# Second layer's experts: a group of h is transposed and evicted one weight piece later

## The reference

```python
g, idx = lax.top_k(jnp.swapaxes(aff, 1, 2), cap)      # cap = 128 tokens for each expert
xe = hf[flat].reshape(b, N_EXPERTS, cap, d)           # gather, d = 1024
a = jnp.einsum('becd,edf->becf', xe, w_gate)          # f = 1408
u = jnp.einsum('becd,edf->becf', xe, w_up)
y = jnp.einsum('becf,efd->becd', jax.nn.silu(a) * u, w_down)
y = y * g[..., None]
out = jnp.zeros((b * n, d), y.dtype).at[flat].add(y.reshape(-1, d))
```

## Time and profile before

| | |
|---|---|
| median of 3 runs | 3465.7 us |
| the profiled execution | 3464.97 us |
| its span (first to last instruction) | 3463.2 us |
| outside the span | 1.8 us |
| mean granted TensorE clock | 0.934 of 2.4 GHz |
| TensorE busy | 3005.9 us (87%) |
| VectorE busy | 2095.8 us (61%) |
| ScalarE busy | 1792.2 us (52%) |

### The profile page before, as it was taken

The page is one execution under the profiler, slowest core; times in us unless marked ns, Lnnn a source line. Parts: engine busy times, 40 slices in busy tenths (PEclk is TensorE's granted clock), DMA queues, the critical chain, the costliest instruction groups (busy, mean ns, idle before and its releaser), DMA issues. The chain is left out here.

```text
span 3463.2 us, 59847 instructions
## 1 busy us (share of the span) xinstructions
PE 3005.9 (87%) x24750; PEld 2458.5 (71%) x24750; DVE 2095.8 (61%) x2213; ACT 1792.2 (52%) x2017; POOL 541.9 (16%) x250
## 2 busy tenths in 40 slices
PE   6599887996799999999999948997929999999993
PEld 2488643452688888788888836774529999999993
DVE  0422375234566666666666645873357888888884
ACT  2411145232555555555555545884336777777773
POOL 1011043001011111210102004561030000000000
PEclk8699889997899999999999969998959999999997
DMA  7211100227778787777788621102247999999995
GB/s 327 75 37 37 55 1 21 85 91 296 274 264 273 263 275 268 259 258 264 270 274 268 239 81 52 40 31 92 93 174 272 362 380 354 354 387 358 354 353 178
DMA packets 137950, 726.07 MB, mean 210 GB/s; under 512 B 10708, under 2 KB 13524, under 8 KB 109828
## 3 DMA queue, kind: packets, MB, share of 16 engines
q1 hardware_dynamic: 125064, 684.99, 52.6%
q0 software_dynamic: 12288, 37.75, 4.6%
q10 hardware_dynamic: 384, 0.24, 0.0%
HBM read 680.90 MB, written 42.04 MB: 209 GB/s over the span
## 5 line engine op out<-in xcount | busy, mean ns | idle before, releaser
L1540 DVE TENSOR_TENSOR mixed_low<-mixed_raw,mixed_high 128x3072 fp32r<-128x3072 f32 (+1 forms) x192 | 593.0, 3092 | 358.8 <-ACT mixed_high L1474 357.8
L1474 ACT CAST mixed_high<-mixed_raw 128x3072 fp32r<-128x3072 f32 (+1 forms) x192 | 489.8, 2554 | 481.2 <-DMA mixed_raw<-in_moe 481.2
L1961 DVE TENSOR_TENSOR rows_low<-rows_raw,rows_high 128x2816 fp32r<-128x2816 f32 x188 | 581.0, 3091 | 80.2 <-ACT rows_high L1905 69.4
L1905 ACT CAST rows_high<-rows_raw 128x2816 fp32r<-128x2816 f32 x188 | 479.4, 2559 | 110.5 <-PE ps L1812 67.1
L1396 PE MATMUL ps<-mixed_high,mixed_xhi 128*128 128x384 f32 (+1 forms) x1024 | 343.7, 336 | 0.5 <-DVE mixed_low L1540 0.5
L1810 PE MATMUL ps<-rows_high,rows_xhi 128*128 128x352 f32 x1024 | 337.4, 330 | 6.0 <-issue 4.5
L1397 PE MATMUL ps<-mixed_low,mixed_xhi 128*128 128x384 f32 (+1 forms) x1024 | 329.9, 322 | 0.0
L1398 PE MATMUL ps<-mixed_high,mixed_xlo 128*128 128x384 f32 (+1 forms) x1024 | 329.9, 322 | 0.0
L1812 PE MATMUL ps<-rows_high,rows_xlo 128*128 128x352 f32 x1024 | 329.8, 322 | 0.0
L1811 PE MATMUL ps<-rows_low,rows_xhi 128*128 128x352 f32 x1024 | 329.5, 322 | 0.0
L1384 PE MATMUL ps<-mixed_raw,mixed_xc 128*32 128x96 f32 (+1 forms) x8192 | 185.3, 243 | 48.3 <-ACT mask_sb L1496 30.8
(11 more groups left out here) (288 smaller groups left out, 5936.3 us busy)
## 6 DMA issues: line engine op xcount, KB each, us to landing
rows_raw<-in_moe_rows SPq DMA_DIRECT2D x192, 1408.0 KB, 7.9
mixed_raw<-in_moe SPq DMA_DIRECT2D x144, 1536.0 KB, 6.7
ring_r<-in_ada_w SPq DMA_DIRECT2D x24, 2048.0 KB, 17.3
mixed_raw<-in_moe SPq DMA_DIRECT2D x48, 1024.0 KB, 6.5
w_raw_r<-in_ev_in SPq DMA_DIRECT2D x18, 512.0 KB, 3.3
w_raw_u<-in_od_in SPq DMA_DIRECT2D x16, 512.0 KB, 3.3
x_res<-ring_r SPq DMA_DIRECT2D x10, 512.0 KB, 2.6
x_norm<-ring_r SPq DMA_DIRECT2D x10, 512.0 KB, 2.9
```

Source lines behind the costliest of these rows:

```text
L1474: act.copy(r.high[:, p % SLOTS, 0:nj, :], r.raw[:, p % SLOTS, 0:nj, :]).then_inc(high_done, 1)
L1540: dve.tensor_tensor(r.low[:, p % SLOTS, 0:nj, :], r.raw[:, p % SLOTS, 0:nj, :], r.high[:, p % SLOTS, 0:nj, :].bitcast(F32), ALU.subtract). ...
L1905: act.copy(high[:, p % SLOTS, :], raw[:, p % SLOTS, :]).then_inc(high_done, 1)
L1961: dve.tensor_tensor(low[:, p % SLOTS, :], raw[:, p % SLOTS, :], high[:, p % SLOTS, :].bitcast(F32), ALU.subtract).then_inc(low_done, 1)
```

## The change

Three `turn` functions are edited; no instruction is added, removed or resized.

- TensorE: inside the loop over units 1 to 3, `turn_h` of the unit before stands after both pieces of the unit instead of between them. So groups 0, 1 and 2 are turned one piece later. Group 3 stays between pieces 0 and 1 of the next turn.
- ScalarE: `copy_h` of groups 0 and 1 moves from places 6 and 8 to places 8 and 10, ahead of `silu` there. Group 2 moves from place 10 to place 0 of the next turn, ahead of `silu`. Group 3 moves from place 0 to place 1.
- VectorE: `split_h` moves likewise. At place 1, the eviction of group 3 stands behind `multiply` of unit 0 in the code, and so behind the split of piece 4 as well, which is place 0.

```diff
--- before.py
+++ after.py
@@ -1880,8 +1880,8 @@
                         turn_x(e + 1)
                 for u in range(1, UNITS) if expert(e) else ():
                     up(e, b, 4 + 2 * u, u, 0)
+                    up(e, b, 5 + 2 * u, u, 1)
                     turn_h(e, u - 1)
-                    up(e, b, 5 + 2 * u, u, 1)
 
             turn_x(0)
             turns(pe, turn)
@@ -1932,13 +1932,15 @@
 
             def turn(e, b):
                 for p in range(TURN):
+                    if p == 0 and later(e):
+                        copy_h(e - 1, 2)
+                    if p in (8, 10) and expert(e):
+                        copy_h(e, p // 2 - 4)
                     if p == 0 or p in (6, 8, 10):
                         if expert(e):
                             silu(e, p, max(0, p // 2 - 2))
-                    if p == 0 and later(e):
+                    if p == 1 and later(e):
                         copy_h(e - 1, 3)
-                    if p in (6, 8, 10) and expert(e):
-                        copy_h(e, p // 2 - 3)
                     if p == 4 and (not isinstance(e, int) or e + 1 < NE):
                         copy_x(e + 1, 1 - b)
                     q = p + SLOTS
@@ -1996,12 +1998,14 @@
 
             def turn(e, b):
                 for p in range(TURN):
+                    if p == 0 and later(e):
+                        split_h(e - 1, 2)
+                    if p in (8, 10) and expert(e):
+                        split_h(e, p // 2 - 4)
                     if p in (1, 7, 9, 11) and expert(e):
                         multiply(e, p, (p - 5) // 2 if p > 1 else 0)
-                    if p == 0 and later(e):
+                    if p == 1 and later(e):
                         split_h(e - 1, 3)
-                    if p in (6, 8, 10) and expert(e):
-                        split_h(e, p // 2 - 3)
                     if p in (3, 5) and later(e):
                         weigh(e - 1, p // 2 - 1)
                     if p == 4 and (not isinstance(e, int) or e + 1 < NE):
```

## The result

The changed kernel took 3541.11, 3528.81, 3534.29 and 3544.37 us, median 3537.7, against 3466.17 us for the kernel before on the same chip. The ratio is 1.021, with a 95% interval from 1.0193 to 1.0226: slower by 2.1%, 71.5 us by the medians. The forecast was 3522 us, slower, with a range from 3500 to 3537: the direction and the place were right, and the size was too small, just outside the range.

A forecast was written before the change was run, and what follows sets the result against it. TensorE was taken to set the pace, VectorE and ScalarE close behind. Waits of 41.3 us plus clock falls of 16.8 less 1.4 made 56.7 us on 3464.97, forecast 3522 us, range 3500 to 3537.

The forecast's parts named there:

- the fourth, the clock: TensorE's granted clock falls behind the new wait before `down` in 12 of 15 turns, 1.4 us each: 16.8 us.
- The waits: Later starts of `down`: 2.54 us in each of 15 turns, 38.1 us, plus 3.2 us in the last turn; 41.3 us.
- What goes: TensorE's wait at group 1's transposes disappears, so it runs 1.80 us ahead towards the turning of group 3.
- The load as anchor: The load ahead of ScalarE's cast stays fixed, so unit 3 comes no earlier; TensorE keeps 0.76 of 1.80 us.
- The wait at down: `down` waits 3.3 us for group 3's low part behind VectorE's chain and starts 2.54 us later each turn.
- the last link: Passing on from the end of VectorE's group 3 eviction to the start of `down`, taken as 0.13 us.
- The last turn: At the stage's final `down`, group 2 and the split of piece 4 now come first: 3.2 us more.
- the fall that goes: The clock fall at 2623 us, behind a 2.58 us wait, disappears with its wait: 1.4 us back.
- The upper bound of 21 us: Upper end for the clock's cost behind the waits before `down`: all 15 turns pay.
- slower still: Rival: loads of pieces 4 and 5 land late, and the clock falls twice in a third of turns; 3544 us, chance 0.07.
- The wait without the clock's fall: Rival: the 3.3 us wait at `down` comes but the clock stays up; 3507 us, chance 0.22.
- Gone, nothing in its place: Rival: the group 1 wait goes and `down` finds group 3 ready; 24.6 us off, 3441 us, chance 0.04.

The follow-up runs named there:

- e6: The kernel before with one edit: VectorE's multiply of unit 1 ahead of the split of piece 10 instead of behind it; 3455.9 us, ratio 0.998.
- e2: The changed kernel with 28 transposes of the identity added ahead of `down`'s first wait to keep TensorE busy; 3509.2 us, ratio 1.0137.
- e7: The kernel before with unit 1's multiply early, and cast and split of piece 8 ahead of the work on the gathered x; 3432.0 us, ratio 0.991.
- e10: The changed kernel with the cast and split of piece 8 ahead of the work on the gathered x; 3522.4 us, ratio 1.0171.
- e1: The changed kernel with group 3's two evictions back at place 0, ahead of the split of piece 4; 3459.9 us, ratio 0.9987.
- e4: The changed kernel with VectorE's eviction of group 3 ahead of unit 0's multiply, still behind the split of piece 4; 3521.7 us, ratio 1.0165.
- e5: The kernel before with only the evictions' part of the change on ScalarE and VectorE, groups turned as before; 3550.5 us, ratio 1.0255.
- e11: The changed kernel with piece 8's cast and split ahead of x and 28 idle transposes ahead of `down`; 3487.0 us, ratio 1.0075.

## Why the prediction was wrong, step by step

The step that failed is the fourth, the clock: it was priced at 15.4 us and cost about 25. The waits, priced at 41.3 us, cost about 46. The direction and the mechanism were right.

**What goes (right).** The 1.64 us wait at group 1 is gone, and unit 3's multiply holds TensorE at group 3 instead: about 1.0 us was said, 1.30 us is in the row above.

**The load as anchor (right, and more than it was used for).** Piece 1's cast keeps its distance of some 35.7 us to `down` in e6, in e2 and, but for the slow clock, in the change. It was called fixed; e7 shows that it is a matter of order. A turn of the kernel before is 1.9 us longer than TensorE's own 48.4; of these e6, which removes the named wait, gets back 0.4, and e7 all.

**The wait at down (right in mechanism, some 5 us too small).** The sum was 41.3 us; e2 has 47 by its ratio, and 46.4 from the first `down` to the end of the profiled span. In the middle of the stage a turn grows from 50.36 to 53.45 us (means of ten turns), 3.1 us and not 2.54. The largest part of this is the last link. From unit 3's multiply to `down` the prediction had 8.09 us; e2 has 3016.03 - 3007.68 = 8.35, and the change 2979.86 - 2971.51 = 8.35 too. VectorE's chain took what was said (7.90 us for 7.96), but between group 3's end and the first matmul of `down` lie 0.44 us (2979.41 to 2979.86 in the change) and not the 0.13 that was read from the transposes. The 0.44 is found wherever `down` waits in its first 14 turns. In the last two it is 0.10 (0.11 in the earlier trace rows):

```profile
3419.65 0.55 DVE L1982 TENSOR_TENSOR rows_htlo<-ps,rows_hthi 128x384 fp32r<-128x384 f32 x1
3420.30 0.55 PE L1810 MATMUL ps<-rows_high,rows_hthi 128*128 128x256 f32 x1 [3.02 <-issue]
```

The 14 turns are those of the kernel's loop (`Fori`), where the values to wait for are worked out in registers; the last two are written out. In the gap that ends at 2979.86 the trace has three instructions of TensorE's own sequencer one after another, two on registers (L1835, L1805) and a further wait (L1806). In the gap that ends at 3420.30 none begins: there the wait at L1806 is a single one that began at 3414.4. That would explain the 0.34 us between them; no run tests it by itself.

The other 0.2 us come from the one turn that was read: it was 0.12 us longer than the mean of the ten, and its multiply 0.09 us earlier behind `down`. The loads, costed at nothing, are left with 0.1: the multiply comes 45.11 us behind `down` in e2 and 45.02 before. The last turn was said to cost 3.2 us more, and in e2 the last interval is 49.30 us against 46.10. The first turn costs nothing, as its own long wait of 2.58 us goes: from the matmul at 2615.53 to the first `down` are 28.4 us before, and 28.3 for the same way in the change. So 14 turns pay and not 15.

**The clock (the step that failed).** "I take 12 of 15, 16.8 us", and 15.4 after the fall that goes. The price of a stretch was right: from the first to the 15th `down` the change has 15 slow stretches more than e2, 17 against 2, and takes 20.9 us more, 1.4 each. The count was wrong. Each of the 15 turns has a fall (in one turn it goes with a wait of 2.68 us at group 3, and `down` waits only 1.80), and four have two stretches in a row: 19 stretches. One goes, that at 2623: 18 by 1.4 is 25.2 us. The last turn adds little: 10.2 us are slow there where it was 6.8, but 5.0 of them lie inside the wait, so that 5.2 us behind it are slow against 4.6 before. Between e2 and the change the profiled executions differ by 25.4 us from the first `down` to the end, the ratios by 25 and the medians by 28.5. The upper bound of 21 us allowed one stretch per wait, so it was no bound. A double fall was kept for the rival "slower still", at 0.07; it came in four turns here, and in 12 turns of e10.

From the first `down` to the end of the span the kernel before takes 819.3 us, e2 865.7 and the change 891.1: 46.4 for the waits and 25.4 for the clock, 71.8 together, and 71.5 was measured by the medians.

The Trainium skill, page "TensorE: Matmul & The Clock Gate", section "HAM oscillation — how this bites in real kernels", says that a kernel whose TensorE stops for data in every iteration pays in every one. The prediction set 12 of 15 against it from the rows. For the waits of 3.3 us the page was the better guide: 15 of 15 turns of the change paid, though one turn of e10 did not. For waits of 1.3 and 1.6 us, which recur just as often, no fall shows in any profile here.

**The other rivals.** The wait without the clock's fall (3507 us) is e2, 3509. "Gone, nothing in its place" was rightly given little: it needs group 3 ahead of the split, which is e1.

## What to carry to other kernels

When a wait moves work later in an engine's list, look at what it moves behind: an eviction that the next stage needs must not pass a long split and an instruction that itself waits for TensorE. Price a new wait of TensorE twice, once for its length and once for the granted clock behind it, and let the upper bound of the second be two slow stretches for each wait. Read a turn's lengths as means of several turns, not from one. Where a wait is named but the turn hangs on a load, removing the wait gives little (e6, 0.4 of 1.64 us) until the load is asked for earlier (e7).

## What the runs showed of the hardware

The counts here are of the profiled execution of each kernel, in this stage, without its last turn. Waits of TensorE of 0.5 to 2.0 us left the granted clock at 1.00. Of 41 waits of 2.2 to 3.02 us, 35 brought it to 1.2 GHz, for 3.4 us, and the longest of them for 6.8; among the six that did not are three of e4's 13 waits of 2.9 us at `down` and one of 2.86 us in e6. Of 42 waits at `down` of 3.28 us and more (in the change, e4, e5 and e10), 41 did, for 3.4 or 6.8 us; the exception is e10's wait of 3.38 us that ends at 2697.91. With 28 transposes of the identity in the wait (e2, e11) no fall followed a `down` before the last turn, nor one in e2's last turn, where 3.45 us of the wait were left idle behind them.

Not expected was that waits of nearly the same length cost one slow stretch or two. e10's are at most 0.1 us longer than the change's, and were followed by two in 12 turns and not in four. What tells the two cases apart in these traces is where the slow time begins. In 76 falls at waits of 2.2 us and more it lasted 6.8 us in the 19 cases in which it began 0.72 us or more before the wait's end, and 3.4 us in the 57 in which it began later (0.68 us before the end at the earliest). In e10's 12 double cases it began 1.0 to 1.4 us before the end. What fixes that moment is not shown by any run.

The stage's start differs between executions though the code is the same up to there: the clock rises between 2590 and 2604 us, and TensorE turns the second expert's x anywhere from 2596 to 2609 us. That is probably part of the spread of some 5 to 20 us in every set of runs; only one execution of each kernel was profiled, so it is not shown.
